# Two-layer hybrid decoder on one core: expert 0 starts on a gather of its own columns, a new order inside each expert, and six banks for the projections

## The reference

```python
for l in range(DEPTH):                       # DEPTH = 2
    proj = x @ w_in[l]                       # 1024 -> columns of all head groups
    o_gla  = gla_mixer(gq, gk, gv, gg, ga, ...)
    o_ssd  = ssd_mixer(sz, sxbc, sdt, ...)   # causal conv over xbc, chunked scan
    o_rwkv = rwkv7_mixer(rwkv_cols, ...)
    x = layer_norm(ALPHA * x + concat(o_gla, o_ssd, o_rwkv) @ w_out[l], ...)
    x = layer_norm(ALPHA * x + grouped_moe(x, ...), ...)

def grouped_moe(x, router_w, router_b, w_gate, w_up, w_down):
    scores = sigmoid(x @ router_w)           # 16 experts in 4 groups
    # best group by the sum of its two best, then the two best experts inside it
    for e in range(16):
        he = silu(h @ w_gate[e]) * (h @ w_up[e])     # 1024 -> 512
        out = out + gate[:, e:e + 1] * (he @ w_down[e])
```

## Time and profile before

| | |
|---|---|
| median of 3 runs | 939.0 us (938.84 to 939.6) |
| the profiled execution, its own time | 938.79 us |
| its span, first to last instruction | 937.1 us |
| mean granted TensorE clock | 0.955 of full |
| TensorE matmul busy | 824.6 us (88%) |
| TensorE weight loads busy | 467.9 us (50%) |
| VectorE, ScalarE, GpSimd busy | 319.3, 180.5, 25.9 us |
| bytes moved | 245.87 MB, mean 262 GB/s |

### The profile page before, as it was taken

One profiled execution on the slowest core, in us unless ns is written; L12 is line 12 of the kernel. 1 busy time (PEld: TensorE's weight loads), 2 busy tenths in 40 slices (PEclk: granted clock), 3 DMA queues, 4 the chain that ended last, 5 costly groups with the idle time before them and its releaser, 6 DMA issues. The chain is left out here.

```text
span 937.1 us, 12772 instructions
## 1 busy us (share of the span) xinstructions
PE 824.6 (88%) x5333; PEld 467.9 (50%) x5333; DVE 319.3 (34%) x671; ACT 180.5 (19%) x380; POOL 25.9 (3%) x102
## 2 busy tenths in 40 slices
PE   4997989986999999898589799999599999998882
PEld 4886566544543444333278685664364444333331
DVE  0195355555211111111243934473722111111115
ACT  1142222422211100000122223232232111000011
POOL 7100000000000000000000000000000000000000
PEclk9998999997999999999879999999789999999997
DMA  9752220245799999999925513010858999999991
GB/s 298 248 180 90 93 89 2 90 183 221 297 423 420 421 421 421 421 421 422 389 87 180 180 58 123 3 59 32 325 182 336 423 421 421 421 421 420 422 379 49
DMA packets 54229, 245.87 MB, mean 262 GB/s; under 512 B 8356, under 2 KB 11280, under 8 KB 29584
## 3 DMA queue, kind: packets, MB, share of 16 engines
q1 hardware_dynamic: 49824, 239.41, 64.1%
q0 software_dynamic: 1344, 4.72, 1.4%
q10 hardware_dynamic: 2992, 0.79, 0.4%
HBM read 243.85 MB, written 1.05 MB: 261 GB/s over the span
## 5 line engine op out<-in xcount | busy, mean ns | idle before, releaser
L481 PE MATMUL bank<-ring,xg 128*64 128x512 f32 x800 | 183.2, 604 | 21.2 <-DMA ring<-in_exp_w_up 19.0
L919 PE MATMUL bank<-x_cm,ring 128*128 128x256 f32 x576 | 134.6, 397 | 17.8 <-DVE xbc L1514 11.3
L919 PEld LDWEIGHTS bank<-x_cm,ring 128*128 128x128 f32 x576 | 114.9, 201 | 37.4 <-DVE xbc L1514 12.3
L481 PEld LDWEIGHTS bank<-ring,xg 128*64 128x64 f32 x800 | 61.4, 139 | 136.2 <-issue 133.2
L672 DVE TENSOR_TENSOR x_cm<-x_cm,bank 128x256 f32<-128x256 f32 x32 | 13.5, 421 | 225.6 <-issue 205.8
L680 DVE TENSOR_TENSOR y_lo<-bank,y_hi 128x512 fp32r<-128x512 f32 x32 | 22.1, 692 | 137.2 <-ACT y_hi L609 137.2
L509 PE MATMUL bank<-ring_more,x_cm 128*64 128x512 f32 x288 | 65.8, 598 | 0.4 <-issue 0.4
L926 PE MATMUL bank<-ring,x_cm 128*128 128x512 f32 x128 | 57.7, 599 | 0.0
L1251 PE MATMUL bank<-ring,x_cm 128*128 128x512 f32 x128 | 55.6, 592 | 0.0
L603 ACT ACTIVATE x_cm<-bank 128x256 f32<-128x256 f32 x32 | 12.3, 384 | 221.9 <-PE bank L494 221.7
L481 PE MATMUL bank<-ring_more,xg 128*64 128x512 f32 x224 | 50.8, 593 | 3.5 <-DMA ring_more<-in_exp_w_up 3.5
(11 more groups left out here) (364 smaller groups left out, 914.2 us busy)
## 6 DMA issues: line engine op xcount, KB each, us to landing
ring<-in_exp_w_gate SPq DMA_DIRECT2D x50, 1024.0 KB, 14.1
ring<-in_exp_w_up SPq DMA_DIRECT2D x50, 1024.0 KB, 16.0
ring_more<-in_exp_w_down SPq DMA_DIRECT2D x36, 1024.0 KB, 17.8
ring<-in_exp_w_down SPq DMA_DIRECT2D x28, 1024.0 KB, 16.3
ring<-in_w_in SPq DMA_DIRECT2D x24, 1024.0 KB, 8.8
ring_more<-in_exp_w_gate SPq DMA_DIRECT2D x14, 1024.0 KB, 14.6
ring_more<-in_exp_w_up SPq DMA_DIRECT2D x14, 1024.0 KB, 16.6
ring<-in_w_out SPq DMA_DIRECT2D x8, 1024.0 KB, 6.9
```

Of the source, the lines that this page charges most:

```text
L481: m = T.matmul(b[SL * i:SL * i + SL, :], xg[g][:, 4 * h + k, cols], w[:, k, :], start=(h == 0 and k == 0), stop=(h == 1 and k == 3))
L919: m = T.matmul(out_, w[:, k, c:c + n], x_cm[:, k, :], start=(k == 0), stop=(k == KD - 1))
```

## The change

1. **Order of the loads.** The halves h = 0 of expert e + 1 are now loaded before the down halves of expert e, and its halves h = 1 behind them.
2. **Order inside a unit.** `down` lags half a unit: `hidden(n, 1)`, `scatter(n - 1)`, `turn(n)`, a gather block, `hidden(n + 1, 0)`, `down(n)`. ScalarE and VectorE are ordered to match.
3. **First half of expert 0.** `pick` is written for the 64 columns of expert 0 first, four blocks are gathered for these columns alone, ScalarE takes them out, and `first_half` does `hidden(0, 0)` ahead of the branch. The gather of the rest (448 columns for blocks 0 to 3, 512 for 4 to 7) moves behind the branch; its first matmul releases the two slots of the first half.
4. **Constant products.** `keep_busy` is a matmul of 256 columns of two constants whose result nobody reads: 7 while VectorE ranks, 3 before the small gather.
5. **Projection banks.** Projections 4 and 7 go to banks 6 and 7, the others alternate as before between 0 and 1 (`proj_bank`; 13 stays in bank 5). The wait of each follows its own bank, so projection 8 now waits for the conv of projection 5 and not for that of 6. The transposes, the gate and projection 9 are put in another order, with VectorE and ScalarE to match.

```diff
+        yield from gate_up(0, 0)
+        for e in range(NE):
+            yield from gate_up(e, 1)
+            if e + 1 < NE:
+                yield from gate_up(e + 1, 0)
+            yield from down(e)
...
+        proj_bank = (0, 1, 0, 1, 6, 0, 1, 7, 0, 1, 0, 1, 0, 5)
...
-                if i < 2:
+                if i in (0, 1, 4, 7):
                     pass
-                elif i - 2 < 8:
-                    pe.wait_ge(*done("v_proj", l, i - 1))
+                elif i < 10:
+                    pe.wait_ge(*done("v_proj", l, (1, 2, None, 3, 4, None, 6, 7)[i - 2]))
...
+        def first_half(pe, l):
+
+            (wg, full_g), (wu, full_u) = slot_w(l, "gate0", 0), slot_w(l, "up0", 0)
+            pe.wait_ge(*full_g)
+            pe.wait_ge(*full_u)
+            for k in range(4):
+                pe.wait_ge(*done("s_first", l, k + 1))
+                for i, w in enumerate((wg, wu)):
+                    T.matmul(b_hid[0][SL * i:SL * i + SL, :], xg[0][:, k, 0:SL], w[:, k, :], start=(k == 0), stop=False)
...
+            def keep_busy(b, n):
+
+                for i in range(n):
+                    T.matmul(bank[b][:, 0:S], ident[:], level_mask[:, 0:4], start=True, stop=True)
...
+                keep_busy(1, 7)
                 pe.wait_ge(*done("v_sel", l))
...
-                pe.wait_ge(*done("v_first", l))
-                for k in range(KD):
-                    if k >= 4:
-                        pe.wait_ge(*done("s_first", l, k - 3))
-                    inc(gather(k, bank[k % 4]), "t_first")
+                keep_busy(1, 3)
+                pe.wait_ge(*done("v_first", l, 1))
+                for k in range(4):
+                    m = gather(k, bank[0][:, k * SL:k * SL + SL], slice(0, SL))
+                inc(m, "t_first")
+                first_half(pe, l)
                 two_ways(pe, l, lambda rounds: experts_t(pe, l, rounds))
...
             for n in range(N):
                 g = n // GU + 1
-                hidden(n, 0)
...
+                hidden(n, 1)
+                if n == 0:
+                    position_rows(0)
+                else:
+                    scatter(n - 1)
+                turn(n)
...
+                if n + 1 < N:
+                    hidden(n + 1, 0)
+                if n == 0:
+                    position_rows(1)
+                pe.wait_ge(*at("v_gcol", min(g + 1, N // GU)))
+                down(n)
```

More of the change, by code:

```diff
@@ L77, in expert_loads, with gate_up @@
     def expert_loads(l):
[L79 to L83, removed]
+        def gate_up(e, h):
+            for kind in ("gate", "up"):
+                src = t[f"exp_w_{kind}"][l, e].rearrange("(p k) f -> p k f", k=KD)
+                yield f"{kind}{e}", h, [(halved(src, h), 0)]
         def down(e):
@@ L540, in position_rows @@
                 inc(m, "t_prow")
-            pe.wait_ge(*done("s_first", l))
             if rounds == 1:
+                pe.wait_ge(*done("v_first", l))
+                pe.wait_ge(*done("s_first", l, 4))
+                for k in range(KD):
+                    if k >= 4:
+                        pe.wait_ge(*done("s_first", l, k + 1))
+                    m = gather(k, bank[k % 4][:, first_cols(k)], first_cols(k), release="t_wgu" if k == 0 else None)
+                    inc(m, "t_first")
+                pe.wait_ge(*done("s_first", l))
                 st.have(pe, "t_gather", GU)
@@ L618, in experts_s @@
             if rounds == 1:
+                for k in range(KD):
+                    act.wait_ge(*done("t_first", l, k + 2))
+                    inc(affine_x1(xg[0][:, k, first_cols(k)], bank[k % 4][:, first_cols(k)], l, k), "s_first")
                 st.have(act, "s_xg", GU)
@@ L978, in _, with turned @@
                     proj(i)
+                def turned(dst, src):
+                    for j in range(TT):
+                        for b in range(2):
+                            m = T.transpose(dst[:, j * RW + b * P:j * RW + b * P + P], src[:, b, tile_(j)], ident[:])
+                    inc(m, "t_turned")
+                pe.wait_ge(*done("v_proj", l, 5))
+                turned(bank[6], rwc[:, 4:6])
                 proj(8)
@@ L1545, in _ @@
                 conv(6)
+                dve.wait_ge(*done("t_proj", l, 8))
+                inc(V.tensor_copy(low[:], bank[7][:, 0:S]), "v_dt")
                 dve.wait_ge(*done("v_ratio", l))
@@ L2080, in _ @@
                 inc(A.activation(rt[:, 1], rt[:, 0], ACT.Exp, scale=-1.0), "s_route")
[L2081 to L2083 removed]
+                act.wait_ge(*done("t_first", l, 1))
+                for k in range(4):
+                    inc(affine_x1(xg[0][:, k, 0:SL], bank[0][:, k * SL:k * SL + SL], l, k), "s_first")
                 two_ways(act, l, lambda rounds: experts_s(act, l, rounds))
```

205 lines of the change are left out of this document (90 added, 115 removed).

## The result

The changed kernel takes 933.0 us (median of 8 runs, 929.8 to 937.3), the kernel before 939.7 in the same session: ratio 0.9929, 95% interval 0.9908 to 0.9950. It is faster by 6.7 us, not by the 16.9 forecast, and outside the range. Its runs also lie 7.5 us apart, those of before 2.0.

A forecast was written before the change was run, and what follows sets the result against it. Two lengths per layer were taken to count: the way to unbroken transfers and the 80 loads behind it. Mixers 16.2, entry 0 and lag 0 gave 16.2 us off 938.79, 922.6, as median 922.8 us; range 917.5 to 930.

The forecast's parts named there:

- Banks and order of the mixers: Mixers: projections 7 and 8 no longer meet the late conv, first pair products 8.1 us earlier per layer, 16.2 in all.
- I take 2.2, nearest to the narrow row: Expert entry: price in us of the small gather's 16 matmuls of 64 columns, chosen between 1.3 and 3.9.
- the upper bound of 3.9: Expert entry: the most the small gather could cost, in us, at the 512-column step of 0.247.
- `first_half`: 3.65, moved, not added: Expert entry: first half of expert 0 takes 3.65 us ahead of the branch, as work moved rather than added.
- Rest of the gather at full clock, 7.4: Behind the branch: the remaining 32 gather matmuls take 7.4 us against 10.39, mostly through the clock the constant products raise.
- Branch 0.5: Expert entry: the branch on TensorE, formerly hidden, now leaves 0 to 1.1 us open; 0.5 taken.
- The rival of the stall: Expert entry: the branch stalls TensorE, 3.1 us more in each layer, 929.0 us; chance 0.06.
- One fall of the clock, 1.85 in each layer: Around slot gates and position rows: the clock falls once, adding 1.85 us and moving the release to 710.4.
- The last pause ends with `hidden(1, 0)`: Expert stage: the first half of unit 1 releases the slots that end the transfers' last pause, at 710.2 us before.
- Tail, "nothing": Stage end: last up half lands 5.0 us later, yet the last scatter ends at 922.05 against 922.14, no gain.
- the entry is dearer: Expert entry: constant products fail to hold the clock or small gather costs 3.9; 3.5 us per layer, 929.8; chance 0.11.
- The clock behind projection 9: Mixers: some 6 us of narrow matmuls bring the clock down, 2.4 us per slow projection, 927.6 us; chance 0.12.

The follow-up runs named there:

- e1: The kernel before with only the new projection banks and the new order in the mixers; 922.9 us, ratio 0.9817.
- e5: The changed kernel without small gather, early first half of expert 0 and constant products, so banks, half-unit lag and load order only; 923.9 us, ratio 0.9831.
- e3: The changed kernel without its constant products; 932.9 us, ratio 0.9914.
- e4: The changed kernel with the small gather's 64 columns streamed eight times, so each of its 16 matmuls has 512 columns; 929.7 us, ratio 0.9875.
- e8: The kernel before with the mixers' part, and both halves of unit 1 moved straight behind those of unit 0; 923.3 us, ratio 0.9817.
- e7: The kernel before with the mixers' part, plus 12 constant products in the ranking and 5 ahead of the old wide gather; 918.6 us, ratio 0.9763.
- e9: The kernel before with the mixers' part, half-unit lag and load order, plus 12 and 5 constant products around the old wide gather; 919.8 us, ratio 0.9780.
- e6: The changed kernel with the small gather made 512 columns wide and 12 constant products in the ranking instead of 7; 930.8 us, ratio 0.9907.

## Why the prediction was wrong

The account in medians: before 940.6, mixers -17.7 (e1), lag +1.0 (e5), own entry +9.0 (e3), products +0.2 gives the 933.0 of the changed kernel. By the ratios, which allow for the 1 us between the medians of before, it is -17.2, +1.3, +7.8 and +1.4. The forecast had -16.2, 0, 0 and 0.

- *Banks and order of the mixers*: right in place, and the size is inside the interval of e1. The profiled executions show 8.3 us a layer from projection 7 to the pairs (forecast 8.1).
- *Small gather, "I take 2.2, nearest to the narrow row"*: the step that failed. It measured 4.0 to 4.2 us, at either clock: the upper bound of 3.9 in the same line. The matmul to compare with was the one that loads the same weights, the 0.247 us of the earlier trace rows. The 0.247 is no price of 512 columns: 448 take 0.24 and 64 take 0.24. It is no price of 128 x 128 weights either, for the narrow products of the forecast have weights of that size too. The nearest row has the small gather's very shape, 128 x 128 weights and 64 columns, in the mixers (L1253), and steps at 0.11 us:

```profile
159.66 1.89 PE L1253 MATMUL bank<-xdt_rows,seg_a 128*128 128x64 f32 x16
161.39 1.95 PE L1253 MATMUL bank<-xdt_rows,seg_b 128*128 128x64 f32 x16
```

  What differs is the load of the weights. By groups, with the count, the busy time and the mean ns of one, in the changed kernel:

```profile
L401 PEld LDWEIGHTS bank<-pick,x_lo 128*128 128x128 f32 x80 | 26.9, 337 | 0.1
L545 PEld LDWEIGHTS bank<-y_hi,pick_t 64*128 64x128 f32 x128 | 12.1, 184 | 31.3 <-issue 30.0
L1253 PEld LDWEIGHTS bank<-xdt_rows,seg_a 128*128 128x128 f32 x32 | 3.9, 192 | 1.0 <-issue 1.0
```

  The gather's load takes 337 ns, that of L1253 192. (L1253 has two rows for each float32 product of the program, so 0.22 us a product; the gather has one.) Two things set the gather's weights apart: the program reads them with a stride of 8 elements (`x[:, j, k::KD]`), and they are declared float32r. Loads of float32r without the stride take 184 ns (L545, 64 rows of weights), which points to the stride; no run changed either, so the cause of the 0.24 stays open. The Trainium skill (TensorE: Matmul & The Clock Gate, LDWEIGHTS) says that a load of weights takes a time that goes with the columns of the stationary tile, by its formula 0.107 us for 128. The step of L1253 is near that figure and loading does not depend on the moving columns here either, but the gather's step is more than twice the figure, and the measurement decides.
- *"`first_half`: 3.65, moved, not added"*: it took 5.07 and 5.35, the second term that failed. The forecast gave a gain to the wide gather for the clock and never asked at which clock the half behind a narrow gather runs. e4 shows that this is the narrow gather's doing.
- *"Rest of the gather at full clock, 7.4"*: 8.15 us, since 448 columns are no cheaper than 512. Full clock was right, but not because of the products (e3).
- *Branch 0.5*: nothing. The first half ended at 679.30 and the first matmul behind the branch began at 679.23. Layer 0 shows the same. The rival of the stall falls for the entry.
- *One fall of the clock, 1.85 in each layer*: beside the one of the first half, which the forecast did not have, there was one in layer 1, 1.7 us at `hidden(0, 1)`, and none in layer 0. e3 has it in both layers, e4 in neither. That it comes and goes is the likely reason for the spread of 7.5 us, whose runs were granted 0.953 to 0.964. No run isolates this.
- *The last pause ends with `hidden(1, 0)`*: holds for the changed kernel, where the order behind it stayed, but not as a rule (e8).
- *Tail, "nothing"*: the last up half came 6.9 us later behind the release in layer 0, worked out were 5.0, as one wait of 2.4 us, and took 5.35 us. Of the 3.6 us missing in the third row of the first table, 1.7 are this slow half and 0.6 lie in the mixers and routing of layer 1. The rest, 1.3, has its like in e5, whose last half of layer 0 took 3.65 us: 1.0 us more than e1 from the release to the last scatter. The medians put lag and load order at 1 us in both layers together.
- *Rivals*: "the entry is dearer" was the case that came, with 3.5 us a layer for some 4.5. Of its two causes the price of the small gather came; the wide gather at a slow clock did not, and the slow first half came in its place. The 3.9 had a row behind it, and 0.11 was too little. The clock behind projection 9 stayed at 1.00; the transposes there did not matter. The Trainium skill (TensorE: Matmul & The Clock Gate, Part 4), by which the prediction held that rival likelier, is not borne out by this trace.

The arithmetic should have warned: sixteen matmuls were added on the way to save one eighth of the columns of sixteen others.

## What to carry to other kernels

Price a narrow matmul by a row that loads the same weights in the same way, and not by one of like shape: look at PEld beside PE in a window. Where PEld was full, as in this gather, cutting columns saved nothing, and splitting the gather paid for the loads of its weights twice. Ask of every group you add what clock it leaves behind for the next one. And when a release is moved to end a pause of the transfers, find the release behind it first; the cheaper version here was the old gather with a few dense products ahead of it, 918.6 us (e7).

## What the runs showed of the hardware

- The clock fell behind a group in which TensorE had no idle time: PE was at 3.00 of 3.00 us in the small gather of layer 1 (670 to 673), with 64 columns a matmul, and the window behind it (674 to 677) was granted 0.50. With 512 columns in the same matmuls it was granted 1.00 there (e4).
- The step of 0.24 us of the gather is the same at a granted clock of 0.50 (e3, 4.01 us for 16 matmuls of 64 columns) and at 1.00 (layer 0 of the changed kernel, 4.00 us). With 512 columns the step does follow the clock: the first twelve matmuls of the wide gather before took 0.44 each at the lower level, 679.69 to 684.97.
- Weights of 128 x 128 have no one price: loads of 337 ns and a step of 0.24 us for the gather's, read with a stride of 8, loads of 192 ns and a step of 0.11 for those of L1253.
- Idle waits of 2.4 us for a transfer were followed by a slow half, 5.33 to 5.35 us, in 4 of 7 cases of the changed kernel; the 22 shorter waits of the old order, 0.3 to 1.3 us, never were. The Trainium skill (TensorE: Matmul & The Clock Gate, HAM oscillation) describes such falls behind waits for transfers; the rows agree, though 3 of the 7 waits had none.
- With 12 and 5 dense constant products the gather was granted 1.00 in e9 (213 to 221 and 664 to 672); without products the gather before was granted 0.50 in its first half (679.7 to 685). What came behind the products differs: a fall at the slot gates in both layers of e6, at the position rows in layer 1 of e7, and none in the entries of e9.
